# Column runs and pass orders in the gate matmuls of a hybrid MLA and mLSTM layer on one core

## The reference

```
p = h @ w_in                       # every branch input is a column block of one projection
y = x + [MLA(h) * silu(z_A) ; mLSTM(h) * silu(z_B)] @ w_out
mLSTM(h) includes sigmoid(mo) * rmsnorm(...)
```

## Time and profile before

| | us |
|---|---|
| median of 3 runs | 2050.56 (2050.15 to 2050.72) |
| profiled execution | 2050.55 |
| its span, first to last instruction | 2048.8 |
| TensorE busy in the span | 2037.7 (99%) |
| VectorE busy | 1109.7 (54%) |
| ScalarE busy | 912.9 (45%) |
| GpSimd busy | 180.1 (9%) |

### The profile page before, as it was taken

One profiled execution on the slowest core, in us unless ns is written; L12 is line 12 of the kernel. 1 busy time (PEld: TensorE's weight loads), 2 busy tenths in 40 slices (PEclk: granted clock), 3 DMA queues, 4 the chain that ended last, 5 costly groups with the idle time before them and its releaser, 6 DMA issues.

```text
span 2048.8 us, 36249 instructions
## 1 busy us (share of the span) xinstructions
PE 2037.7 (99%) x15059; PEld 2007.7 (98%) x15059; DVE 1109.7 (54%) x1995; ACT 912.9 (45%) x1826; POOL 180.1 (9%) x206
## 2 busy tenths in 40 slices
PE   9999999999999999999999999999999999999999
PEld 9999999999999999999999999999999999999999
DVE  5545767676555445455555555444555654444444
ACT  5644455565444334344444444444444543343443
POOL 0001033333200000000000011000000000000000
PEclk9999999999999999999999999999999999999999
DMA  9655443333455454645545555555555556665554
GB/s 244 189 171 155 119 118 106 97 102 119 123 171 145 137 165 124 177 129 166 144 144 166 165 166 165 167 171 167 168 169 162 169 178 187 188 188 188 185 184 134
DMA packets 197436, 323.28 MB, mean 158 GB/s; under 512 B 21392, under 2 KB 68136, under 8 KB 197272
## 3 DMA queue, kind: packets, MB, share of 16 engines
q1 hardware_dynamic: 195160, 317.45, 53.4%
q10 hardware_dynamic: 2112, 3.51, 0.5%
HBM read 310.11 MB, written 9.62 MB: 156 GB/s over the span
## 4 chain that ended last, share of the span: by engine, by line
PE 96%; ACT 2%; DVE 1%; issue 1%; DMA 0%; SPq 0%; DVEq 0%; ACTq 0%
PE bank L1682 29%; PE bank L1685 29%; PE bank L1686 29%; PE bank L1945 1%; PE bank L1847 1%; PE bank L1846 1%; PE bank L1844 1%; PE bank L1910 1%; PE bank L1911 1%; ACT whi L731 0%; PE bank L2147 0%; ACT rsb L823 0%; PE bank L1707 0%; PE bank L2030 0%; ACT rsb L821 0%
## 5 line engine op out<-in xcount | busy, mean ns | idle before, releaser
L1136 DVE TENSOR_TENSOR wlo<-raw,whi 128x512 fp32r<-128x512 f32 (+1 forms) x1256 | 819.7, 662 | 878.6 <-ACT whi L731 875.6
L1682 PE MATMUL bank<-xhi,whi 128*128 128x288 f32 (+2 forms) x4128 | 1231.4, 298 | 0.1
L1685 PE MATMUL bank<-xlo,whi 128*128 128x288 f32 (+2 forms) x4128 | 1222.0, 296 | 0.0
L1686 PE MATMUL bank<-xhi,wlo 128*128 128x288 f32 (+2 forms) x4128 | 1221.9, 296 | 0.0
L731 ACT CAST whi<-raw 128x512 fp32r<-128x512 f32 (+1 forms) x1256 | 708.2, 577 | 974.0 <-PE bank L1686 938.7
L1682 PEld LDWEIGHTS bank<-xhi,whi 128*128 128x128 f32 (+1 forms) x4128 | 774.7, 188 | 2.6 <-issue 1.1
L1685 PEld LDWEIGHTS bank<-xlo,whi 128*128 128x128 f32 (+1 forms) x4128 | 774.9, 188 | 1.6 <-issue 1.0
L1686 PEld LDWEIGHTS bank<-xhi,wlo 128*128 128x128 f32 (+1 forms) x4128 | 774.5, 188 | 0.0
L1682 PE MATMUL bank<-cqhi,whi 128*128 128x288 f32 x288 | 89.5, 311 | 1.2 <-DVE wlo L1136 0.6
L1685 PE MATMUL bank<-cqlo,whi 128*128 128x288 f32 x288 | 84.8, 294 | 0.0
L1686 PE MATMUL bank<-cqhi,wlo 128*128 128x288 f32 x288 | 84.8, 294 | 0.0
(11 more groups left out here) (314 smaller groups left out, 1283.7 us busy)
## 6 DMA issues: line engine op xcount, KB each, us to landing
raw<-in_w_in_dram SPq DMA_DIRECT2D x313, 512.0 KB, 3.8
raw<-in_w_out_dram SPq DMA_DIRECT2D x128, 512.0 KB, 3.7
raw<-in_w_in_dram SPq DMA_DIRECT2D x146, 256.0 KB, 3.1
raw<-in_w_q_up_dram SPq DMA_DIRECT2D x48, 384.0 KB, 3.3
raw<-in_w_kv_up_dram SPq DMA_DIRECT2D x16, 512.0 KB, 3.6
xres<-in_x_prompt_dram SPq DMA_DIRECT2D x16, 256.0 KB, 4.0
out_dram<-ytok SPq DMA_DIRECT2D x15, 256.0 KB, 4.2
xt<-in_x_prompt_dram SPq DMA_DIRECT2D x7, 384.0 KB, 9.9
```

The costliest lines, as they stand in the source:

```text
L1136: ins = tt(lo, src, hi.bitcast(f32), ALU.subtract)
L1682: ins = mm(out, w_hi, m_hi, start=start, stop=False, **kw)
L1685: mm(out, w_hi, m_lo, start=False, stop=False, **kw)
L1686: return mm(out, w_lo, m_hi, start=False, stop=stop, **kw)
```

## The change

A new function `gate_group` takes the place of `group` for the ten groups of phase `gates`. It has the same waits and releases, the same weight tiles and the same number of matmuls. Two groups keep the old order. Eight differ from it in one way each, or in two:

- group 1 reads the columns and writes the bank in runs of 2: all pairs at columns 4n, 4n+1, then all at 4n+2, 4n+3 (144 runs)
- group 2 takes the passes in the order hi*hi, lo*hi, hi*lo
- group 3: runs of 8, alternating between the two halves of the 288 columns (36 runs)
- group 4: pass by pass, each pass over the four column tiles, in place of tile by tile
- group 5: runs of 16, every second block of 16 first (18 runs)
- group 6: the passes in the order hi*lo, hi*hi, lo*hi
- group 7: runs of 48 (6 runs, in the order 0, 2, 4, 1, 3, 5)
- group 8: pass by pass in the order hi*hi, lo*hi, hi*lo
- groups 9 and 10: as before

The same reordering is applied to the moving operand and to the output, so each result lands in its old place.

```diff
--- before.py
+++ after.py
@@ -1708,6 +1708,43 @@
                              c("ident" if t else "perm", n)[:, 0:n])
                 ins.then_inc(full[b], 1)
 
+            def as_stored(v):
+                return v
+
+            def runs_of_2(v):
+                return v.rearrange("p (n s t) -> p s n t", s=2, t=2)
+
+            def runs_of_16(v):
+                return v.rearrange("p (n s t) -> p s n t", s=2, t=16)
+
+            def runs_of_8(v):
+                return v.rearrange("p (h n t) -> p n h t", h=2, t=8)
+
+            def runs_of_48(v):
+                return v.rearrange("p (a b n) -> p b a n", a=3, b=2)
+
+            def gate_group(g, phase, i, b0, order=as_stored, passes=(0, 1, 2), by_pass=False):
+
+                u = U_GATE + g * KT
+                for k in range(KT):
+                    pe.wait_ge(lo_done, u + k + 1)
+                    hi, lo = order(xhi[:, k, N_META:NT]), order(xlo[:, k, N_META:NT])
+                    todo = [(ct, n) for ct in ((0, 1, 2, 3) if k else (0, 2, 1, 3)) for n in range(3)]
+                    if by_pass:
+                        todo.sort(key=lambda x: x[1])
+                    for at, (ct, n) in enumerate(todo):
+                        if k == 0 and n == 0:
+                            fill(phase, b0 + ct, 0, i)
+                        w, m = ((whi, hi), (whi, lo), (wlo, hi))[passes[n]]
+                        ins = mm(order(bank[b0 + ct][:, 0:NQ]), w[:, k % HL_SLOTS, ct * P:ct * P + P], m,
+                                 start=k == 0 and n == 0, stop=k == KT - 1 and n == 2)
+                        if k == 0 and at == 0:
+                            ins.then_inc(unit_used, 1)
+                        if k == KT - 1 and n == 2:
+                            ins.then_inc(full[b0 + ct], 1)
+                    if k < KT - 1:
+                        ins.then_inc(unit_used, 1)
+
             def group(u, phase, nth, i, c0, hooks=lambda k: None, a_hi=xhi, a_lo=xlo, ready=None, x_ready=False,
                       queries=0, b0=0, turn=(0, 2, 1, 3), mixed=False):
 
@@ -2131,9 +2168,15 @@
                 group(U_ML + 3 * KT + h * (2 * KT), "ml", 1, h, 0)
             group(U_GATE, "gate0", 0, 0, N_META, mlstm("gate0", 0, 3))
 
+            GATE_ORDERS = ((dict(order=runs_of_2), dict(passes=(0, 2, 1))),
+                           (dict(order=runs_of_8), dict(by_pass=True)),
+                           (dict(order=runs_of_16), dict(passes=(1, 0, 2))),
+                           (dict(order=runs_of_48), dict(by_pass=True, passes=(0, 2, 1))),
+                           (dict(), dict()))
             for g in range(0, 5):
-                group(U_GATE + KT + g * (2 * KT), "gates", 0, g, N_META, b0=4)
-                group(U_GATE + 2 * KT + g * (2 * KT), "gates", 0, g, N_META)
+                odd, even = GATE_ORDERS[g]
+                gate_group(2 * g + 1, "gates", g, 4, **odd)
+                gate_group(2 * g + 2, "gates", g, 0, **even)
 
             group(U_GATE + 11 * KT, "gate11", 0, 0, N_META, b0=4)
             group(U_OUT, "out0", 0, 0, N_META, a_hi=mhi, a_lo=mlo, mixed=True, ready=mix_lo)
```

## The result

The changed kernel takes 2101.57 us in the median of 4 runs (2101.26 to 2102.02) against 2050.36 for the kernel before in the same comparison. The ratio is 1.025, 95% interval 1.0235 to 1.0266: slower by 51.2 us.

A forecast was written before the change was run, and what follows sets the result against it. TensorE was taken as the bound, 131.6 ns per matmul in the gate groups. Orders, tile by tile and runs each added 0, giving 2050.6 us, with a range from 2049 to 2095 us.

The forecast's parts named there:

- the one on runs: Groups 1, 3, 5 and 7: reading and writing the 288 columns in shorter runs adds 0 us.
- The row it leaned on: V columns' matmuls, moving operand with one jump in 256 columns: 119.2 ns against 116.7 without; 0 to 2.5 ns per jump.
- Rival 1: Group 1: runs of 2 go at half rate, one column in two clocks, adding 43 us: 2093.6 us; chance 0.17.
- Rival 4: All short runs slow, runs of 8 and 16 at half rate too: 129 us, 2180 us; chance 0.04.
- the leftover: Rival that the leftover, not explained in the text given, grows: 2055 us; chance 0.07.
- a price per jump: Rival that each jump between runs in the reordered groups costs time: 2083 us; chance 0.12.
- something gets faster: Case that the changed kernel gets faster, no size given in the text; chance 0.06.
- The orders: Changed order of passes (groups 2 and 6) and pass by pass (groups 4 and 8) were to cost 0 us.
- tile by tile: Groups 4 and 8, pass by pass instead: a bank change at every matmul, in place of every third, costs 0.
- The end of group 4: First bank's last matmul comes 0.8 us later, so VectorE ends at most 0.8 us later, covered by 2.3 us slack.
- The helpers: ScalarE's wait for TensorE stays near 285 us, growing by just what a slower group adds.

The follow-up runs named there:

- swapped pairs: Changed kernel, but group 1 reads and writes columns 2, 3, 0, 1, then 6, 7, 4, 5, both pairs of a line successively: 2053.95 us against 2050.44.

## Why the prediction was wrong

**The step that failed** is the one on runs, which stands in the sum as 0. That 0 was the author's estimate, the low end of the 0 to 2.5 ns per jump that the earlier trace rows leave open, and no run shows it for these patterns. What the runs showed in its place: for runs of 2 the price is 125.0 ns per matmul and 48.0 us, for 8, 16 and 48 together 3.2 us. The kernel with swapped pairs shows that a new run inside a line is free (143 jumps, 131.7 ns), and the changed kernel that two reads of a line are not enough (256.6 ns). A line costs some 1.8 ns each time it is entered, whether two columns of it are read (256.6 ns over 144 entries) or four (131.7 over 72), and that is a little more than four columns take at the least rate of the runs, 0.425 ns each (122.5 / 288), 1.70 ns in all. The row it leaned on the earlier trace rows has 128 columns between jumps, that is 32 full lines, and could not show this. The prediction ends on a run of 2 as what no row of before can exclude, and the range was to carry the doubt.

**The rivals.** Rival 1, half rate for pairs, was the right mechanism in kind: 0.891 ns per column (256.6 / 288) against the 0.846 taken from the plain float32 scores, which is twice the least rate of the float32r columns (0.425). Its estimate, 43 us, was 5 us too low, and the range ended 1.4 us above its value (2093.6), with nothing added for the other runs; so 2101.6 fell outside 2095. With each line read twice or four times over, 288 columns take 122.6 and 122.5 ns, so some 9 of the 131.7 ns are there only when every line is read once. Rival 4 fails at group 3 (136.7 ns, not 243.5).

The range also rests on 2055 for the leftover and on 2083 for a price per jump, both the author's estimates, and no run shows the term of either. What the runs showed in their place: a price per jump (0.12) is excluded by the swapped pairs (143 jumps, 131.7 ns), and the growth in group 1 is 48.0 us and goes with how often a line is entered. That something gets faster (0.06) fails with 131.7 ns in groups 4 and 8.

**The orders** were right: 0 for the passes, 0 for tile by tile. The end of group 4 went as worked out too. VectorE's rows there, in the timeline of the kernel after:

```profile
1324.70 1.54 DVE L1605 TENSOR_TENSOR gt<-bank,rB 128x288 f32<-128x288 f32 x4
1327.27 3.90 DVE L1136 TENSOR_TENSOR wlo<-raw,whi 128x512 fp32r<-128x512 f32 x4 [1.02 <-ACT whi L731]
```

Group 5 starts at 1324.77, so the four banks are read from 0.07 us before it, where they were read from 0.86 us before it: 0.8 us later, and so is the next remainder. The waits of TensorE in the whole kernel show that none of it reaches TensorE; no line of the gate groups stands there:

```profile
PE bank L1776 <- DMA con<-in_shape_table_dram: 4.1, 1, 4.1
PE bank L1682 <- DVE wlo L1136: 1.2, 2, 0.6
PE bank L2077 <- DVE kwh L1526: 1.1, 4, 0.3
```

**The helpers** were to wait longer by what a slower group adds: ScalarE's wait for TensorE went from 285 us to 329.7 over a stretch 50 us longer, 45 of the 51 us.

What stays open: why every fourth column (288 lines entered, 260.0 ns) costs hardly more than every second (144, 256.7), and why runs of 4 begun one column earlier took 269.9 ns, which neither the count of lines nor that of pairs gives; what makes the jumps of groups 3, 5 and 7 cost 1.7 to 5.0 ns; and by what rule the place where a run begins moves it from 130.0 to 135.6.

## What to carry to other kernels

With a float32r moving operand, order the columns as you like as long as all four columns of an aligned 16 bytes are read close together: the patterns tried in runs whose start and length are multiples of 4 columns stay within 7% of one long run (131.7 to 140.0 ns), and runs of 2 that break every line take 256.6 ns, about half the rate of the 131.7 of one long run. The orders of passes, weight tiles and banks tried here, and the output in runs of 2, 8, 16 and 48, were free (131.7 ns). When the nearest row of a profile is far from the shape at hand, let the range reach past the price of the worst plausible rival and add the small ones to it.

## What the runs showed that was not expected

- A matmul of 288 columns took as little as 122.5 to 124.2 ns, 0.425 to 0.431 ns per column, only where lines were read more than four times each; one plain pass over 72 lines takes 131.7.
- The reader keeps at least four neighbouring 16-byte lines: four in turn, one column each, gave 124.0 ns, eight gave 246.6.
- Storing the normalised and the mixed activations 4 bytes off a 16-byte line, with no other difference in the kernel, cost the kernel 44.7 us (2.2%); 12 bytes off it cost nothing and 60 bytes off 10.3 us.
